# Part one's mixers in one block: in-projection, HGRN, mLSTM, banded attention and out-projection of a two-part transformer kernel

## The chip, the cores and the metric

The kernel runs on one core of one Trainium2 chip. The metric is the time of one execution on the device in microseconds (us); every time below is from the profile, the timed runs or the trace of one profiled execution. Engines: PE is TensorE, DVE is VectorE, ACT is ScalarE, POOL is GpSimd, SP issues the DMAs.

## The reference, cut to what matters

Two models follow one another on x (512 tokens, width 1024, fp32), each with two layers. Only part one's mixers are touched:

```python
for l in range(2):                       # first_block
    y = rms_norm(x) @ w_in[l] + b_in[l]  # 1024 -> 2824 columns
    # mq mk mv mo: 4 heads of 64; mi mf: 4 each; hq hf hi hg: 4 heads of 64
    # sq: 8 heads of 64, sk sv: 2 heads of 64
    qk    = silu(causal_conv4(mq|mk))
    m_out = head_norm(mlstm(qk, mv, mi, mf)) * sigmoid(mo)
    h_out = head_norm(hgrn2(silu(hq), hf, hi)) * silu(hg)     # decays exp(G_l - G_s), per feature
    s_out = banded_attention(rope(norm(sq)), rope(norm(sk)), sv, window 128, sinks)
    x = x + concat(m_out, h_out, s_out) @ w_out[l]
    x = x + square(relu(rms_norm(x) @ w_up[l])) @ w_down[l]   # 4096 wide
    x = x + gate(...)                                          # embedding gate
# second_block: two layers with three attentions and a gated MLP (5632 -> 2816)
```

## The kernel before, in words

**Products.** A weight matrix is cut into panels of at most 128 x 2048 fp32 (1 MB). SP loads a panel into one of `RAW` (3) buffers. ACT copies it rounded into one of three `high` buffers (`Panels.high`, L297), DVE puts the remainder into `low` (`Panels.low`, L309), and PE forms each product as three (high x high, high x low, low x high). `AHEAD` is 2: panel n+2 is split when work on panel n starts. `Panels.loads` lets the load of panel n wait until panel n-RAW has been split. A *feature group* is 24 matmuls of 128x512 (`project_feature`, L426), a *token group* 24 matmuls of 128x256 (`project_token`, L451). In part one's MLP the panels of `w_mod_2` are not split: DVE itself multiplies them (L1427, L1430), one beside each of the panels 1 to 6 of every eight.

**Part one's mixers** (`layer_one`, `mixers_one`, `project_heads`) are five stages, one block after the other. All engines meet between blocks.

1. In-projection: norm, then 12 panels in 9 feature and 28 token groups over six PSUM banks. Beside them DVE and ACT make the convolution and the gate sums.
2. mLSTM: 16 blocks (head, key tile). PE spreads the running maximum (L1041) and makes the scores (L1047), DVE adds the mask (L1097) and multiplies (L1106), ACT takes exp (L1069), PE sums over values (L1058). HGRN's gates are made beside them.
3. HGRN: two head pairs, ten levels each. Level lv cuts the tokens into blocks of 2B. `prepare` makes the spans of G against the middle of each block (L1151, then the sign L1153), ACT takes exp (L1223), `decay` multiplies all 512 queries and all 512 keys (L1164, L1165), PE makes 8 products (L1261), `keep` picks them under a mask (L1176). POOL rotates the window's queries and keys meanwhile. At a pair's end PE makes the results (L1237). Then queries and keys are turned (L555, L558).
4. Window attention: 32 units (head, query tile): scores (L467), maximum (L501), exp (L529), transposes (L478), copy (L538), result (L488), copy (L515).
5. Head scaling (L876, L882) and `project_heads`: transposes (L615), then 8 feature groups, each added to x (L886).

Part two's mixers (`layer_two`) are one block already: dense groups stand between the steps of attention pairs (`dense_at`), two heads of a pair use different rows of the array (L1821), and the dense groups use two banks.

Of the kernel before, what the change touches and what calls it, by code (L numbers as in the profile page):

```python
# [14 lines left out]
F32 = mybir.dt.float32  # L15
# [6 lines left out]
P = 128  # L22
# [7 lines left out]
RAW = 3  # L30
# [26 lines left out]
V_WIDTH = 64 + 6 * DC  # L57

R_BIAS, R_GM, R_GH, R_GQK, R_SINK = 0, 1792, 2048, 2304, 2944
# [19 lines left out]
def panels_one():  # L79


    k = lambda name, c0, n=PW: (name, 0, DC, [(c0, n, 0)], n)
    out = [k("w_in", 0), k("w_in", 256), ("w_in", 0, DC, [(C_GATES, MH, 0), (C_GATES + MH, MH, 32)], P)]
    out += [k("w_in", c) for c in (C_HQF, C_HQF + 256, C_MVO, C_MVO + 256, C_HIG, C_HIG + 256, C_SQ, C_SQ + 256, C_SKV)]
    out += [k("w_out", c) for c in range(0, D, PW)]
# [63 lines left out]
class AttentionSignals:  # L149
# [9 lines left out]


class TurnSignals:
    def __init__(self, s, name):
        self.t_ready = s(name)
        self.t_kept = s(name + "_kept")


class Unit:


    def __init__(self, q, k, cols, mask, scale, col, values, out, at=0, extra=None, sink=None):  # L170
        self.q, self.k, self.cols, self.mask, self.scale = q, k, cols, mask, scale
        self.col = col
        self.values, self.out = values, out
        self.at = at
        self.extra, self.sink = extra, sink
# [283 lines left out]
def attention_tensor(nc, pe, g, s, units):  # L459
    n = len(units)  # L460
    for i in range(n + 2):
        if i < n:
            u = units[i]
            if i >= 2:
                pe.wait_ge(s.max_ready, i - 1)
            b = g.bank[i % 2][:, 0:u.cols]
            ins = nc.tensor.matmul(b, u.q, u.k, start=True, stop=u.extra is None)  # L467
            if u.extra is not None:
                ins = nc.tensor.matmul(b, u.extra[0], u.extra[1], start=False, stop=True)
            ins.then_inc(s.scores_ready, 1)  # L470
        if 1 <= i <= n:
            j = i - 1
            u = units[j]
            pe.wait_ge(s.probs_ready, j + 1)
            if j >= 2:
                pe.wait_ge(s.turned_kept, j - 1)
            for m in range(u.cols // P):
                ins = nc.tensor.transpose(g.bank[2 + j % 2][:, m * P:(m + 1) * P], g.probs[:, j % 3, m * P:(m + 1) * P], g.ident)  # L478
            ins.then_inc(s.turned_ready, 1)
        if i >= 2:  # L480
            j = i - 2
            u = units[j]
            pe.wait_ge(s.turned_kept, j + 1)
            if j >= 2:
                pe.wait_ge(s.out_kept, j - 1)
            nb = u.cols // P
            for m in range(nb):
                ins = nc.tensor.matmul(g.bank[4 + j % 2][:, 0:2 * HD], g.turned[:, j % 2, m * P:(m + 1) * P], u.values[m],  # L488
                                       start=m == 0, stop=m == nb - 1)
            ins.then_inc(s.out_ready, 1)  # L490


def attention_vector(nc, dve, g, s, units):
    n = len(units)
    for i in range(n + 2):
        if i < n:
            u = units[i]
            dve.wait_ge(s.scores_ready, i + 1)
            if i >= 3:
                dve.wait_ge(s.probs_ready, i - 2)  # L500
            nc.vector.tensor_tensor_reduce(out=g.masked[:, i % 3, 0:u.cols], in0=g.bank[i % 2][:, 0:u.cols], in1=u.mask,  # L501
                                           scale=1.0, scalar=NEG, op0=ALU.add, op1=ALU.max,
                                           accum_out=g.rowmax[:, u.col:u.col + 1]).then_inc(s.max_ready, 1)
            dve.wait_ge(s.max_ready, i + 1)
            if u.sink is None:
                nc.vector.tensor_scalar(g.negmax[:, u.col:u.col + 1], g.rowmax[:, u.col:u.col + 1], -u.scale, None,
                                        ALU.mult).then_inc(s.neg_ready, 1)
            else:
                nc.vector.tensor_scalar(g.negmax[:, u.col:u.col + 1], g.rowmax[:, u.col:u.col + 1], u.sink, -u.scale,
                                        ALU.max, ALU.mult).then_inc(s.neg_ready, 1)  # L510
        if i >= 2:
            j = i - 2
            dve.wait_ge(s.out_ready, j + 1)
            at = units[j].at
            nc.vector.tensor_copy(units[j].out, g.bank[4 + j % 2][:, at:at + HD]).then_inc(s.out_kept, 1)  # L515


def attention_scalar(nc, act, g, s, units, beside=None):

    n = len(units)  # L520
    for i in range(n + 1):
        if i < n:
            u = units[i]
            if beside is not None:
                beside(i)
            act.wait_ge(s.neg_ready, i + 1)
            if i >= 3:
                act.wait_ge(s.turned_ready, i - 2)
            nc.scalar.activation(g.probs[:, i % 3, 0:u.cols], g.masked[:, i % 3, 0:u.cols], ACT.Exp,  # L529
                                 bias=g.negmax[:, u.col:u.col + 1], scale=u.scale,  # L530
                                 accum_out=g.rowsum[:, u.col:u.col + 1]).then_inc(s.probs_ready, 1)
        if i >= 1:
            j = i - 1
            act.wait_ge(s.turned_ready, j + 1)
            if j >= 2:
                act.wait_ge(s.out_ready, j - 1)
            c = units[j].cols
            nc.scalar.activation(g.turned[:, j % 2, 0:c], g.bank[2 + j % 2][:, 0:c], ACT.Copy).then_inc(s.turned_kept, 1)  # L538


def attention_buffers(nc, ctx, g, part):
    g.masked = ctx.enter_context(nc.sbuf_tensor(part + "_masked", [P, 3, S], F32))
    g.probs = ctx.enter_context(nc.sbuf_tensor(part + "_probs", [P, 3, S], F32))
    g.turned = ctx.enter_context(nc.sbuf_tensor(part + "_turned", [P, 2, S], F32))


def turn_tensor(nc, pe, g, s, blocks):

    for i, srcs in enumerate(blocks):
        if i >= BANKS:  # L550
            pe.wait_ge(s.t_kept, i - BANKS + 1)
        for m, src in enumerate(srcs):
            to = g.bank[1 + i % BANKS][:, m * P:(m + 1) * P]
            if src.shape[1] == P:
                ins = nc.tensor.transpose(to, src, g.ident)  # L555
            else:
                for r in range(0, P, HD):
                    ins = nc.tensor.matmul(to[r:r + HD, :], src, g.ident, start=True, stop=True)  # L558
        ins.then_inc(s.t_ready, 1)


def turn_scalar(nc, act, g, s, outs):
    for i, out in enumerate(outs):
        act.wait_ge(s.t_ready, i + 1)
        nc.scalar.activation(out, g.bank[1 + i % BANKS][:, :], ACT.Copy).then_inc(s.t_kept, 1)

def project_heads(nc, g, part, s, pan, l, columns, steps, before_scalar, before_vector, update):  # L570


    first = pan.first["w_out"]
    grp = Groups(["turn"] * DC + ["x"] * DC, {"turn": s("mix_low"), "x": s("x_updated")})
    full, high_ready = s("out_products"), s("mix_high")
    e = NormSignals(s, "mlp")
    with ExitStack() as ctx:
        mh = ctx.enter_context(nc.sbuf_tensor(part + "_mix_high", [P, DC, S], F32R))
        ml = ctx.enter_context(nc.sbuf_tensor(part + "_mix_low", [P, DC, S], F32R))
        with nc.Block() as block:  # L580
            @block.sync
            def _(sp):
                pan.loads(sp, l, first + AHEAD, first + 4 + AHEAD)

            @block.vector
            def _(dve):
                before_vector(dve)
                for c in range(DC):
                    dve.wait_ge(high_ready, c + 1)
                    nc.vector.tensor_tensor(ml[:, c, :], grp.bank(g, c)[:, :], mh[:, c, :].bitcast(F32), ALU.subtract).then_inc(s("mix_low"), 1)  # L590
                for c in range(DC):
                    if c % 2 == 0:
                        pan.low(dve, first + c // 2 + AHEAD)
# [1800 lines left out]
```

## Time and profile before

| | before |
|---|---|
| timed runs, us | 3276.65 median of 3 (3272.84 to 3308.1) |
| the profiled execution | 3276.12 us, its span 3274.3 us |
| PE / DVE / ACT / POOL busy | 3001.4 / 1696.6 / 1120.3 / 183.1 us |
| mean granted TensorE clock | 0.914 of full |

"Busy" is the time in which an instruction of that engine was under way; matmuls are pipelined and their ends are modelled, so a busy PE is not PE at its peak. The granted clock is the share of 2.4 GHz that the chip let TensorE have.

### The profile page before, as it was taken

Reading aid. Unit: us, or ns where it says so; the run is one execution under the profiler, and the core shown is the slowest. Engines: PE = TensorE matmul, PEld = TensorE weight load, DVE = VectorE, ACT = ScalarE, POOL = GpSimd, SP = SyncE. Lnnn points to the kernel's source line nnn. Section 1 sums busy time; section 2 is a strip of 40 time slices with the busy share of each in tenths; the row PEclk is TensorE's granted clock in tenths of the full one; section 3 lists DMA queues with packets and bytes.
Section 4 is the critical chain, followed back from the end, with each engine's and each line's share of the span. In section 5 each row is a group of like instructions: output and inputs, shape, how many; then the busy total and the mean of one; then the engine's idle time right before and its main releaser. Section 6 shows DMA issues by size and latency. Waiting matters only on the chain. (4 is left out here: it accounts for less than half of the span.)

```text
span 3274.3 us, 38168 instructions
## 1 busy us (share of the span) xinstructions
PE 3001.4 (92%) x14756; PEld 2451.6 (75%) x14756; DVE 1696.6 (52%) x2899; ACT 1120.3 (34%) x1851; POOL 183.1 (6%) x184
## 2 busy tenths in 40 slices
PE   5977899999889789999997899989999998999998
PEld 4956678888678576788886687778887787778886
DVE  3458555566553754655565553454342643454442
ACT  3252532223433424322234434433232434342231
POOL 0012000000200120000002000000000000000000
PEclk9955899999989556999998899999999999999999
DMA  4200034444142000344441310122321310122321
GB/s 167 94 13 1 14 116 155 154 155 167 33 143 78 1 1 14 123 161 160 160 155 34 127 64 28 39 79 77 115 80 51 136 51 28 52 78 79 108 87 61
DMA packets 42994, 281.39 MB, mean 86 GB/s; under 512 B 5944, under 2 KB 6200, under 8 KB 11704
## 3 DMA queue, kind: packets, MB, share of 16 engines
q1 hardware_dynamic: 42808, 278.86, 24.3%
q8 instruction: 122, 2.00, 0.2%
q14 instruction: 64, 0.52, 0.1%
HBM read 276.75 MB, written 2.10 MB: 85 GB/s over the span
## 5 line engine op out<-in xcount | busy, mean ns | idle before, releaser
L309 DVE TENSOR_TENSOR low_panels<-raw_panels,high_panels 128x2048 fp32r<-128x2048 f32 (+3 forms) x218 | 469.4, 2153 | 359.6 <-ACT high_panels L297 359.5
L297 ACT ACTIVATE high_panels<-raw_panels 128x2048 fp32r<-128x2048 f32 (+3 forms) x218 | 392.2, 1800 | 538.9 <-PE bank L1369 196.0
L426 PE MATMUL bank<-mlp_h_high,high_panels 128*128 128x512 f32 x1152 | 456.9, 397 | 0.0
L426 PE MATMUL bank<-mlp_h_low,high_panels 128*128 128x512 f32 x1152 | 454.9, 395 | 0.0
L426 PE MATMUL bank<-mlp_h_high,low_panels 128*128 128x512 f32 x1152 | 454.9, 395 | 0.0
L426 PEld LDWEIGHTS bank<-mlp_h_high,low_panels 128*128 128x128 f32 x1152 | 215.9, 187 | 52.8
L426 PEld LDWEIGHTS bank<-mlp_h_low,high_panels 128*128 128x128 f32 x1152 | 216.0, 188 | 51.8
L426 PEld LDWEIGHTS bank<-mlp_h_high,high_panels 128*128 128x128 f32 x1152 | 216.0, 188 | 51.7
L1369 PE MATMUL bank<-mlp_hid_high,high_panels 128*128 128x512 f32 x512 | 204.4, 399 | 0.0
L1369 PE MATMUL bank<-mlp_hid_low,high_panels 128*128 128x512 f32 x512 | 202.4, 395 | 0.0
L1369 PE MATMUL bank<-mlp_hid_high,low_panels 128*128 128x512 f32 x512 | 202.3, 395 | 0.0
L1430 DVE SCALAR_TENSOR_TENSOR mlp_mod_acc<-raw_panels,conditioning,mlp_mod_acc 128x256 f32<-128x256 f32 x336 | 165.1, 491 | 12.0
L1934 ACT ACTIVATE masked_scores<-masked_scores,stats 128x128 f32<-128x128 f32 (+3 forms) x160 | 81.3, 555 | 219.3 <-DVE stats L2038 219.3
L1261 PE MATMUL bank<-one_turned,one_probs 64*128 64x128 f32 (+1 forms) x512 | 99.9, 453 | 42.9 <-DVE one_probs L1165 42.9
L2161 PE MATMUL bank<-mlp_hid_high,low_panels 128*128 128x512 f32 x352 | 139.0, 395 | 0.0
L2161 PE MATMUL bank<-mlp_hid_high,high_panels 128*128 128x512 f32 x352 | 139.0, 395 | 0.0
L2161 PE MATMUL bank<-mlp_hid_low,high_panels 128*128 128x512 f32 x352 | 139.0, 395 | 0.0
L343 ACT ACTIVATE norm_buffers<-x 128x512 f32<-128x512 f32 x88 | 55.3, 630 | 242.4 <-DVE x L1451 66.4
L352 POOL TENSOR_TENSOR norm_buffers<-norm_buffers 128x512 f32<-128x512 f32 x11 | 16.3, 1480 | 2178.5 <-ACT norm_buffers L343 2178.5
L426 PE MATMUL bank<-h_high,high_panels 128*128 128x512 f32 x320 | 133.0, 416 | 0.2
L426 PE MATMUL bank<-h_low,high_panels 128*128 128x512 f32 x320 | 127.5, 398 | 0.0
L1261 PEld LDWEIGHTS bank<-one_turned,one_probs 64*128 64x128 f32 x512 | 86.9, 324 | 54.1 <-DVE one_probs L1165 53.4
(370 smaller groups left out, 5970.3 us busy)
## 6 DMA issues: line engine op xcount, KB each, us to landing
raw_panels<-in_w SPq DMA_DIRECT2D x238, 1024.0 KB, 4.9
raw_panels<-in_w SPq DMA_DIRECT2D x16, 384.0 KB, 3.2
raw_panels<-in_w SPq DMA_DIRECT2D x4, 960.0 KB, 4.7
raw_panels<-in_w SPq DMA_DIRECT2D x4, 768.0 KB, 4.2
row<-in_row SPq DMA_DIRECT2D x2, 1476.0 KB
x<-in_xT SPq DMA_DIRECT2D x1, 2048.0 KB, 7.5
raw_panels<-in_w SPq DMA_DIRECT2D x4, 512.0 KB, 7.7
mix<-in_rope SPq DMA_DIRECT2D x2, 1024.0 KB, 8.7
```

Of the source, the lines that this page charges most:

```text
L297: self.nc.scalar.activation(self.g.high[:, i % SPLIT, 0:raw.shape[1]], raw, ACT.Copy).then_inc(self.high_ready, 1)
L309: self.nc.vector.tensor_tensor(self.g.low[:, i % SPLIT, 0:w], raw, self.g.high[:, i % SPLIT, 0:w].bitcast(F32), ALU.subtract).then_inc(sel ...
L343: nc.scalar.activation(g.sq[:, c % 2, :], src, ACT.Square).then_inc(e.sq_ready, 1)
L352: nc.gpsimd.tensor_tensor(total, g.sq[:, 0, :], g.sq[:, 1, :], ALU.add).then_inc(e.sum_used, 2)
L426: ins = nc.tensor.matmul(bank[:, :], w[a][:, k, c0:c0 + P], rhs[b][:, k0 + k, :], start=first and k == 0 and j == 0, stop=last and k == kt ...
L1261: ins = nc.tensor.matmul(b[:, o:o + w], k[:, sx * P:(sx + 1) * P], q[:, t0 * P:t1 * P], start=True, stop=True)
L1369: ins = nc.tensor.matmul(b[:, :], w[a_][:, k, (m % 2) * P:(m % 2 + 1) * P], (uh, ul)[b_][:, k, :], start=k == 0 and j == 0, stop=k == DC - ...
L1430: ins = nc.vector.scalar_tensor_tensor(o, w[:, k, :], g.cond[:, k:k + 1], o, ALU.mult, ALU.add)
L1934: nc.scalar.activation(o, o, ACT.Exp, bias=g.negmax[:, 2 * i + m:2 * i + m + 1], scale=u.scale).then_inc(w.probs_ready, 1)
L2161: ins = nc.tensor.matmul(b[:, :], w[a_][:, k, (c % 2) * P:(c % 2 + 1) * P], (uh, ul)[b_][:, k0 + k, :], start=part == 0 and k == 0 and q = ...
```

## The change

Part one's mixers become one block per layer, written as part two's: each engine walks through one list of steps, and dense groups stand between them. `RAW` goes from 3 to 2 in the whole kernel. The dense groups use two banks (1 and 2): group i waits until group i-2 is evicted.

- **Order of the panels.** Forget, query, HGRN input, the two convolution panels, gates, mLSTM values, window keys and values, window queries (2), both gates of the outputs; then w_out as four panels of 4 row tiles x 512 columns.
- **Before the levels** (`n_before` = 8 groups): forget, query, HGRN input. ACT opens forget and query straight from PSUM (Abs, Sigmoid, Silu) and makes the logarithms; DVE scans.
- **Levels** (20 steps). The spans and the decay products are made for half of the tokens each: keys of the first half of a block, queries of the second, so that four operations of 256 elements take the place of four of 512. PE alternates between the two heads' rows. The two coarsest levels' copies go to ACT. Nine dense groups stand between the steps.
- **mLSTM** (16 steps): 20 token groups between them. The rotation moves from POOL to DVE, the squares of the heads stay on ACT.
- **Window attention in pairs** (16 pairs in 19 steps): DVE, ACT and PE as in part two, sinks and normalisation per pair. The eight mixed chunks are turned as they become ready, and 8 half groups of w_out ("first", 12 matmuls) stand between the steps; 8 more ("second") follow.
- Head gains are applied with the turned chunks, no longer by POOL.

The core of the diff (the order, and the loops of the three engines around the levels):

```diff
-RAW = 3
+RAW = 2
+        n_before = 8
+        dense_h = {1: [8], 3: [9], 5: [10], 7: [11], 9: [12], 11: [13], 13: [14], 15: [15], 17: [16]}
+        dense_m = {}
+        for i, j in enumerate(range(17, 37)):
+            dense_m.setdefault(2 * i // 3 if i < 12 else i - 4, []).append(j)
+        dense_w = {i: [first_groups[c]] for c, i in enumerate((7, 8, 9, 10, 12, 13, 16, 17))}
+        chunk_w = {2: [2], 3: [3], 5: [0], 6: [1], 7: [4], 11: [5], 15: [6], 18: [7]}
+        def dense_bank(i):
+            return bank[1 + i % 2]
...
+            @block.tensor            # products(k): waits d_decayed(k), and d_kept(k - 2)
+                for k in range(n_levels):
+                    products(k)
+                    if k == NL + 1:
+                        results(0)
+                    for i in dense_h.get(k, []):
+                        dense(i)
+                for j in range(n_blocks):
+                    if j == 2:
+                        results(1)
+                    if kt == 0:
+                        spread(hd)
+                    block_scores(j)
+                    if kt == 2 and hd >= 1:
+                        block_result(hd - 1)
+                    for i in dense_m.get(j, []):
+                        dense(i)
...
+                for p in range(n_pairs + 3):
+                    scores(p); result(p - 2); turn(p - 1)
+                    for c in chunk_w.get(p, []): turn_chunk(c)
+                    for i in dense_w.get(p, []): dense(i)
+                for i in second_groups: dense(i)
...
+            @block.scalar
+                for i in range(n_before):
+                    evict(i)
+                    if i == 1: forget_logs()      # Exp, Exp, Ln
+                    if i == 3: bound_logs()       # Abs, Abs, Exp, Ln
+                for k in range(n_levels):
+                    decay(k)                      # exp of the span of level k
+                    if k >= 1: keep_apart(k - 1)
+                    for i in dense_h.get(k, []): evict(i)   # waits for the group when ACT evicts it
+                    if k == 11: gate_logs()
+                    if k == 13: conv_open()
...
+            @block.vector
+                for i in range(n_before):
+                    evict(i)                      # at a panel's first group: pan.low(n + AHEAD)
+                    if i == 1: forget_sums(0)
+                    if i == 4: forget_sums(1)     # two scans, a memset
+                for k in range(n_levels):
+                    if k + 1 < n_levels: prepare(k + 1)
+                    decay(k)
+                    if k >= 1: keep(k - 1)
+                    if k == NL + 2: gather(0)
+                    for i in dense_h.get(k, []): evict(i)   # waits for the group when DVE evicts it
+                    if 9 <= k < 9 + CONV1: conv(k - 9)
+                    if k == 10: gates(0)
+                    if k == 14: gates(1)
...
+                def prepare(k):
+                    nc.vector.tensor_tensor(out[:, :, 0:B], ref, blk[:, :, 0:B], ALU.subtract)
+                    nc.vector.tensor_tensor(out[:, :, B:2 * B], blk[:, :, B:2 * B], ref, ALU.subtract).then_inc(s("d_span"), 1)
+                def decay(k):
+                    dve.wait_ge(s("d_decay"), j + 1)
+                    nc.vector.tensor_tensor(out[:, :, 0:B], out[:, :, 0:B], kv[:, :, 0:B], ALU.mult)
+                    nc.vector.tensor_tensor(out[:, :, B:2 * B], out[:, :, B:2 * B], qv[:, :, B:2 * B], ALU.mult).then_inc(s("d_decayed"), 1)
```

Groups 8 to 12 (convolution and gates, k = 1 to 9) are feature groups that ACT evicts; groups 13 to 16 (k = 11 to 17) are token groups that DVE evicts. The loops above are shortened; conditions on the first and last steps are left out.

## Rows read from the trace of the kernel before

**Rows 1.** The page: busy tenths of PE and granted clock in 40 slices.

```profile
PE   5977899999889789999997899989999998999998
PEclk9955899999989556999998899999999999999999
```

**Rows 2.** Stages of layer 0, layer 1's mixers, its window stage (start:end length, busy, PEclk).

```profile
36.00:176.60 140.60, 134.81 (x904) 124.60 (x904) 67.69 (x83) 45.48 (x44) 0.00 (x0) 1.00 0.36 126
176.60:233.00 56.40, 43.61 (x121) 27.26 (x121) 31.66 (x78) 27.39 (x45) 2.39 (x5) 0.52 0.00 1
233.00:339.00 106.00, 79.32 (x416) 71.39 (x416) 76.31 (x119) 33.05 (x112) 30.39 (x40) 0.51 0.00 1
339.00:388.50 49.50, 46.17 (x232) 30.61 (x232) 26.75 (x129) 35.40 (x163) 4.95 (x4) 0.97 0.00 1
388.50:444.10 55.60, 49.57 (x232) 42.01 (x232) 25.56 (x32) 17.44 (x21) 7.75 (x6) 0.94 0.22 76
908.00:1337.70 429.70, 375.96 (x1904) 312.14 (x1904) 228.06 (x440) 159.37 (x383) 45.47 (x55) 0.73 0.14 49
1211.90:1281.40 69.50, 66.94 (x232) 44.84 (x232) 26.73 (x129) 35.47 (x163) 4.95 (x4) 0.61 0.00 1
```

**Rows 3.** Timeline of one HGRN level (start, length in us).

```profile
265.50 3.09 PE L1261 MATMUL bank<-one_turned,one_probs 64*128 64x128 f32 x16 [0.65 <-DVE one_probs L1165]
266.57 0.68 DVE L1151 TENSOR_TENSOR norm_buffers<-proj 128x512 f32<-128x512 f32 x1
268.01 0.63 ACT L1223 ACTIVATE one_masked<-norm_buffers 128x512 f32<-128x512 f32 x1 [3.11 <-DVE norm_buffers L1153]
268.50 0.68 DVE L1165 TENSOR_TENSOR one_probs<-proj,one_masked 128x512 f32<-128x512 f32 x1
269.10 1.32 DVE L1176 COPY_PREDICATED proj<-k,bank 128x512 f32<-128x512 int32 x2
```

**Rows 4.** Timeline of DVE: evictions of two token groups, then two feature groups.

```profile
161.52 0.42 DVE L833 TENSOR_TENSOR proj<-bank,row 128x256 f32<-128x256 f32 x1 [2.46 <-PE bank L451]
164.40 0.42 DVE L833 TENSOR_TENSOR proj<-bank,row 128x256 f32<-128x256 f32 x1 [2.46 <-PE bank L451]
405.33 0.69 DVE L886 TENSOR_TENSOR x<-x,bank 128x512 f32<-128x512 f32 x1 [0.56 <-PE bank L426]
410.77 0.69 DVE L886 TENSOR_TENSOR x<-x,bank 128x512 f32<-128x512 f32 x1 [4.75 <-PE bank L426]
```

**Rows 5.** Timeline of part two: scores of one pair, 4 matmuls of 256 columns.

```profile
1936.74 0.92 PE L1821 MATMUL bank<-q_and_k 32*128 32x256 f32 x8
```

**Rows 6.** Timeline of ACT: a table load between Exp and Ln.

```profile
109.85 0.63 ACT L757 ACTIVATE neg_max<-neg_max 4x512 f32<-4x512 f32 x1
110.50 1.28 ACT L758 ACT_TABLE_LOAD   x1
111.79 0.63 ACT L758 ACTIVATE neg_max<-neg_max 4x512 f32<-4x512 f32 x1
```

**Rows 7.** Stretches of part two's mixers and of layer 1's first matmuls, with clock.

```profile
1900.00:1994.00 94.00, 92.83 (x685) 81.19 (x683) 43.25 (x140) 36.60 (x76) 0.00 (x0) 1.00 0.16 51
1994.00:1998.60 4.60, 2.48 (x23) 2.08 (x22) 3.79 (x9) 2.09 (x4) 0.00 (x0) 1.00 0.02 4
1998.60:2002.00 3.40, 3.40 (x13) 2.91 (x12) 0.83 (x5) 2.36 (x5) 0.00 (x0) 0.50 0.00 0
914.40:920.00 5.60, 5.53 (x13) 4.40 (x14) 5.05 (x6) 2.95 (x3) 0.00 (x0) 0.50 0.58 217
```

**Rows 8.** Timeline of PE in mLSTM and HGRN results, at the low clock.

```profile
202.36 4.61 PE L1047 MATMUL bank<-norm_buffers 64*128 64x512 f32 x6
222.60 4.53 PE L1058 MATMUL bank<-scratch,proj 128*128 128x65 f32 x20
329.93 1.49 PE L1237 MATMUL bank<-proj,scratch 128*128 128x64 f32 x6
```

**Rows 9.** Timeline of part one's MLP, and the landing time of its panel loads.

```profile
570.70 1.91 ACT L297 ACTIVATE high_panels<-raw_panels 128x2048 fp32r<-128x2048 f32 x1
571.91 3.61 DVE L1430 SCALAR_TENSOR_TENSOR mlp_mod_acc<-raw_panels,conditioning,mlp_mod_acc 128x256 f32<-128x256 f32 x7
575.43 2.28 DVE L309 TENSOR_TENSOR low_panels<-raw_panels,high_panels 128x2048 fp32r<-128x2048 f32 x1
DMA to landing us min/median/max: 4.7/5.2/5.9
```

More of the change, by code:

```diff
@@ L453, in project_token @@
     return ins
[L459 to L490, printed above, removed]
@@ L493, in attention_vector @@
[L493 to L515, printed above, removed]
@@ L518, in attention_scalar @@
[L518 to L538, printed above, removed]
@@ L541, in attention_buffers @@
[L541 to L559, printed above, removed]
@@ new lines, in layer_one @@
+        groups += [(12 + c // 4, "first", c) for c in range(DC)] + [(14 + c // 4, "second", c) for c in range(DC)]
+        panel_done = [sum(n <= p for n, _, _ in groups) for p in range(16)]
+        by_act = [sum(gr[1] in ("query", "conv", "gates") for gr in groups[:i]) for i in range(len(groups) + 1)]
+        by_dve = [sum(gr[1] in ("forget", "token") for gr in groups[:i]) for i in range(len(groups) + 1)]
+        by_sum = [sum(gr[1] in ("first", "second") for gr in groups[:i]) for i in range(len(groups) + 1)]
@@ new lines, in released, with level_bank, level_kept @@
+        def released(eng, i):
+            if i < 0:
+                return
+            if groups[i][1] in ("query", "conv", "gates"):
+                eng.wait_ge(kept_a, by_act[i + 1])
+            elif groups[i][1] in ("forget", "token"):
+                eng.wait_ge(kept_v, by_dve[i + 1])
+            else:
+                eng.wait_ge(x_updated, by_sum[i + 1])
+        def level_bank(k, hh_):
+            return bank[3 + (2 * k + hh_) % 4]
+        def level_kept(eng, k):
+            within = levels[k][1] <= TILE_LEVELS
+            n = 2 * sum((lv <= TILE_LEVELS) == within for _, lv in levels[:k + 1])
+            eng.wait_ge(d_kept if within else ao_kept, n)
@@ new lines, in _ @@
+                dve.wait_ge(s("in_gains"), 16)
+                norm_vector(nc, dve, g, e, x, vec[:, V_GIN:V_GIN + DC], hh, hl,
+                            before={1: lambda: pan.low(dve, 0), 4: lambda: pan.low(dve, 1)})
+                dve.wait_ge(s("in_vectors"), 48)
+                bounds(0)
+                st(nc.vector.memset(qk_raw[:, :, 0:3], 0.0))
+                bounds(1)
+                for i in range(n_before):
+                    evict(i)
+                    if i == 1:
+                        forget_sums(0)
+                    if i == 4:
+                        forget_sums(1)
@@ new lines, in _ @@
+                keep(n_levels - 1)
+                gates(2)
+                for j in range(n_blocks + 1):
+                    if j < n_blocks:
+                        block_weights(j)
+                    if j >= 1:
+                        block_probs(j - 1)
+                    if j == 3:
+                        gather(1)
+                    if j in (7, 11, 15):
+                        finish((j - 7) // 4)
+                    for i in dense_m.get(j, []):
+                        evict(i)
+                    if j == 8:
+                        head_squares(hi_out, 0, region(3592, 1024))
+                    if 11 <= j < 15:
+                        rotate(j - 11)
```

1315 lines of the change are left out of this document (685 added, 630 removed).

## The prediction, as put on record before the result

> **What bounds the kernel now.** I read the page's slices first [rows 1]: PE is busy nearly everywhere, and the granted clock is at its full level (2.4 GHz) except in two dips, slices 3 to 5 and 14 to 16, which are the mixers of part one's two layers. The table of stages [rows 2] then says what each stage is worth. The reader is to see three things there. The in-projection (140.6 us) is PE at full clock with idle DVE and ACT. mLSTM and HGRN (56.4 + 106.0 us) have the clock at half and PE waiting: this is where overlap could pay. The window stage costs 49.5 us in layer 0, where the clock stayed up, and 69.5 us in layer 1, where it did not. From the norm's first work to the last sum into x the mixers take 408.1 us in layer 0 (36.0 to 444.1) and 429.7 us in layer 1, together 837.8 us. Nothing outside these stretches is edited, apart from RAW. I price four new phases per layer by the program order of the diff, at full clock first, then with the clock.
>
> **Prices.** One HGRN level is 3.7 us of DVE (0.7 + 0.6 + 0.6 + 0.6 + 1.2) while PE needs 3.1 us at the low clock and ACT 0.63 [rows 3]. An operation of 512 elements takes 0.68 and the next starts 0.60 after it [rows 3]; one of 256 elements takes 0.42 [rows 4], 0.34 by the same overlap. So the halved level costs DVE 4 x 0.34 + 1.2 = 2.6 us. A token group is 2.88 us and a feature group 5.44 us [rows 4]. Level products: two heads on different rows overlap in part two, 4 matmuls of 256 columns in 0.92 us [rows 5], where one after another they would take 1.5 (the 3.1 us of a level's 8 x 128 columns at the low clock, halved); so 0.9 us a level at full clock, 1.8 at the low one. A table load is 1.28 us [rows 6].
>
> **Phase A, up to the first decayed level.** The first two groups end 20.0 us after the start, as now. Then two banks replace six, and group 2 waits for ACT and DVE: bounds with two table loads (3.0), the high copy (1.9), Abs 0.6, a load 1.3, Sigmoid 0.6, DVE 0.6, which is 6.7 us of idle PE. Two query groups 10.9, two token groups 5.8. Group 6 needs group 4 evicted, and before that DVE takes a `low` whose `high` stands on ACT behind the bound logarithms (Silu 0.6, two Abs 1.1, Exp and Ln of 1024 with two loads 4.7, the copy 1.9), then 2.3 + 0.4: some 5.5 us more of idle PE. Two token groups 5.8 and the chain evict, prepare, exp, decay 2.4. Sum 57 at full clock; the two gaps bring the low clock, which costs 3 to 7 more. I take 61, bounds 57 and 64. Here the Trainium skill would say more: ScalarE: Activation LUTs, "What ACT_TABLE_LOAD costs", puts a switch at 2.66 us, a load of 1.28 and a drain of 1.38. The trace disagrees with the second half: Exp ends at 110.48, the load starts at 110.50 and Ln at 111.79 [rows 6], and six loads by the page would make phase A 8 us longer.
>
> **Phase B, the levels.** What matters is who waits for a dense group. At k = 1, 3, 5, 7, 9 ACT evicts it, and the exp of level k+1 stands behind that on ACT. So from decay(k): products 0.9, dense 5.5, PE's tail 0.2, evict 0.6, exp 0.6, decay 0.7, and then the even level's DVE work keep, prepare, decay 2.6: 11.1 us per two levels, 56 for five. At k = 11 to 17 DVE evicts, and prepare and decay of k+1 stand behind: 0.9 + 2.9 + 0.2 + 0.4 + 1.3 + 2.6 = 8.3 us per two levels, 33 for four. On top, not covered by anything: three of four convolution steps 3 x 2.6, the second gate step 4.6 (two scans), results(0) 40 records of 0.21 us at the low clock [rows 8], 4.3 at full, the gather 0.6, the last level's products 0.9. Sum 107. DVE alone would need 20 x 2.6 + 10 + 5 + evictions and lows of about 13 = 80, PE 39 + 18 + 4: neither bounds it, the round trip does. **The clock.** Per two levels PE idles 2.2 us, works 0.9, idles 1.7. In part two a stretch of 4.6 us with 2.1 us idle was followed by a stretch at half clock [rows 7], and layer 1's first full-row matmuls ran 5.6 us at half clock before it rose [rows 7]. So I let each dense group start low: 1.9 to 2.9 us for the group and 0.5 for products, 3.3 x 9 = 30. B is 137; bounds 107 and, low all the way, 158 (5 x 6.3 + 4 x 3.8 + 4.3 more).
>
> **Phase C, mLSTM.** PE: 20 x 2.88 = 57.6; scores 9 (5.4 - 0.6 for a head at the low clock, halved, x 4) and spreads 4; results of three heads 3 x 2.2 and results(1) 4.2 [rows 8]. Sum 81. DVE has 16 x 1.0 + 8 + five lows 11.5 + four rotations of 3 + squares and ends 7 = 55 of these, but crowded in steps 8 to 15, and two banks give little slack: 5 more, 86. PE is over 90% busy, so the clock should hold. The rotation that POOL did beside DVE costs 12 us of DVE here, under cover of token groups; without that cover it would be 12. Bounds 81 to 92.
>
> **Phase D, window and out-projection.** Turning queries and keys 7 (6.7 us with the last results now, between rows 2's HGRN stage and its end). A unit of the window stage takes 1.44 us on average (49.5 us less its ends, 32 units), limited by its chain of engines; a pair needs the same chain once with two heads: 2.9 us, over 18 steps 52. A "first" group is 2.7 us of PE, of which some 0.8 hides in each step: 8 x 1.9 = 15. Steps 1 and 3 carry DVE's head norms (7.5) behind Sigmoid, Silu and Sqrt with four table loads: 12. Chunks 5. Eight "second" groups 22. Sum 113, bounds 105 (chain shorter, as twice 1.33) and 133 (+20, what the low clock does to the stage in layer 1 [rows 2]).
>
> **RAW.** With two raw buffers the load of a split panel starts when the `low` of the panel before it in that buffer ends. In the MLP's crowded periods of 11.65 us that is 6.2 us after the first modulation product, it lands 4.7 to 5.9 later [rows 9], at 10.9 to 12.1; `high` is wanted at 10.8 and ends by 14.0, and the `low` is due only at 15.5, behind the next 3.9 us of modulation. So the slack is 1.5 us and the price zero. In part two the period is 10.9 us with one panel and the slack is larger.
>
> **Sum.** 61 + 137 + 86 + 113 = 397 a layer, 794 for both against 837.8: 43.8 us less. The profiled execution took 3276.1 us (its span 3274.3), within 0.6 us of the median 3276.65, so 3276.1 - 43.8 = 3232.
>
> **Rivals.** (1) *The clock holds at full*, as it does in nearly all of part two's mixers, which have the same form (1.00 over 94 us [rows 7]). Then A is 57, B 107, C 81, D 105: 350 a layer, 3138 us. For it: bursts of 6.4 us, longer than the waits. TensorE: Matmul & The Clock Gate, section "HAM oscillation", has the oscillation arise where bursts are shorter than the waits between them; by that the clock would hold here, and the result would be this rival's. Against it: 2.1 us of idle time in 4.6 sufficed [rows 7]; B has 3.9 in 4.8. (2) *Slower: the clock stays at half through the levels and the pairs*, as it did for the whole of layer 1's window stage although PE counted as busy for 66.94 of 69.50 us [rows 2]. B 158, D 133, A 64, C 88: 443 a layer, 3324 us. It decides against the change from 22 us a layer above my sum, that is when half of what lies between my B and D and these ends is lost. Against it: in layer 1's start dense work brought the clock up after 5.6 us [rows 7], and the dense groups are such work. (3) *Panels become late.* If with two raw buffers a load landed later than 7.4 us after its start, each us over is paid in 48 periods; 8.5 us would give 3232 + 53 = 3285. Two loads already share the queue now and land within 5.9. (4) *The phases overlap as planned but ACT's or DVE's fixed order costs more than my chains*, some 20 us a layer: 3272.
>
> **How the numbers follow.** My forecast 3232 (reach 3190 to 3275) 0.50; rival 1 (3110 to 3190) 0.22; rival 2 0.14; rival 3 0.04; rival 4 0.10. Two in ten may be left out: the range is 3135 to 3310. A measurement of this kernel tells about 1% from no change. Faster by over 1% (below 3244): 0.22 + 0.38 = 0.60; within 1%: 0.12 + 0.10 + 0.02 = 0.24; slower: 0.16.
>
> **What would show it.** After, two levels with a feature group between them are 11 to 15 us apart and PE's idle time there goes to the decayed products of DVE, whose own wait goes to ACT's exp; the clock in the levels is 0.6 to 0.8 on average; the third group of each layer starts some 6 us after the second ends; C has PE busy over 90% at full clock; panel loads land as before and MLP periods stay at 11.65 us. I am wrong if the exp of level k+1 is found ahead of the dense group, if the clock holds, if ACT's table loads in the window steps make a pair longer than 3 us, or if MLP periods grow.

## The result and the profile after

The changed kernel takes 3254.47 us (median of 20 runs, one of which, at 9696 us, stands apart), the kernel before 3282.97 (20 runs, taken beside them); the ratio is 0.9931, 95% interval 0.9906 to 0.9957. That is a gain of 0.7%, which I would have called no change, where I forecast 1.4%. The time lies inside my range. The profiled execution took 3257.54 us (span 3255.7), 18.6 less than that of before.

The page of the changed kernel, busy tenths of PE and granted clock in 40 slices:

```profile
PE   4779889999967788999997998999998998999998
PEclk9769789999988888999998999999999999999999
```

Against [rows 1] the two deep dips are gone. In their place stand longer, shallower ones: 0.6 to 0.9 in slices 2 to 6, 0.8 in 12 to 16. The stages, start:end length, busy time of each engine, and PEclk after the five engines; layer 0, then layer 1, each cut at the first work after the norm, the first level's products, the first spread of mLSTM, the turning of the window's queries, the first "second" group, and the last sum into x:

```profile
35.70:95.80 60.10, 43.71 (x200) 37.17 (x200) 32.25 (x43) 34.56 (x37) 0.00 (x0) 0.86 0.32 115
95.80:229.40 133.60, 95.12 (x554) 79.94 (x553) 70.09 (x138) 32.59 (x45) 0.00 (x0) 0.72 0.09 32
229.40:335.70 106.30, 98.79 (x623) 84.38 (x621) 48.28 (x107) 31.69 (x108) 0.00 (x0) 0.87 0.15 50
335.70:429.40 93.70, 76.79 (x428) 60.01 (x429) 51.90 (x198) 43.03 (x104) 0.00 (x0) 0.80 0.07 23
429.40:454.00 24.60, 23.98 (x107) 18.76 (x105) 11.06 (x12) 8.82 (x11) 7.75 (x6) 1.00 0.25 85
915.60:973.80 58.20, 40.93 (x200) 34.51 (x200) 32.24 (x43) 34.97 (x37) 0.00 (x0) 0.83 0.33 112
973.80:1099.00 125.20, 86.01 (x553) 71.51 (x552) 69.95 (x138) 32.60 (x45) 0.00 (x0) 0.78 0.10 34
1099.00:1200.10 101.10, 93.62 (x622) 80.76 (x621) 48.21 (x107) 31.67 (x108) 0.00 (x0) 0.92 0.15 53
1200.10:1292.30 92.20, 73.31 (x428) 56.69 (x429) 51.86 (x198) 43.06 (x104) 0.00 (x0) 0.85 0.07 24
1292.30:1316.60 24.30, 23.67 (x105) 18.46 (x104) 11.01 (x12) 8.60 (x10) 7.75 (x6) 1.00 0.25 86
```

| us | predicted | layer 0 | layer 1 |
|---|---|---|---|
| A, up to the first level | 61 | 60.1 | 58.2 |
| B, levels | 137 | 133.6 | 125.2 |
| C, mLSTM | 86 | 106.3 | 101.1 |
| D, window and out-projection | 113 | 118.3 | 116.5 |
| sum | 397 | 418.3 | 401.0 |
| before [rows 2] | | 408.1 | 429.7 |

819.3 us against 837.8: 18.5 us less, all of the 18.6 of the whole execution. So on balance nothing moved outside the mixers, and the question is what stands in them: B waits as foreseen, C is 15 to 20 us too long.

One period of two levels in B, layer 1 of the changed kernel, timelines of PE, DVE and ACT (L695 products, L1147 and L1148 decayed products, L1162 keep, L1136 and L1137 prepare, L925 exp):

```profile
1013.54 1.65 PE L695 MATMUL bank<-arena 64*128 64x128 f32 x16 [2.09 <-DVE arena L1148]
1016.09 2.08 PE L695 MATMUL bank<-arena 64*128 64x128 f32 x16 [0.91 <-DVE arena L1148]
```
```profile
1012.72 0.42 DVE L1147 TENSOR_TENSOR arena<-arena 128x256 f32<-128x256 f32 x1 [6.46 <-ACT arena L925]
1013.06 0.42 DVE L1148 TENSOR_TENSOR arena<-arena 128x256 f32<-128x256 f32 x1
1013.40 1.33 DVE L1162 COPY_PREDICATED arena<-k,bank 128x512 f32<-128x512 int32 x2
1014.62 0.41 DVE L1136 TENSOR_TENSOR arena<-arena 128x256 f32<-128x256 f32 x1
```
```profile
1012.07 1.14 ACT L925 ACTIVATE arena<-arena 128x512 f32<-128x512 f32 x2
```

PE ends its feature group at 1011.4 and waits 2.09 us, the tail, ACT's eviction, the exp and the decayed product, one behind the other, exactly the 0.2 + 0.6 + 0.6 + 0.7 of the prediction. DVE, which had been idle for 6.46 us beside the dense group, could have made that product long before: its input waited on ACT behind the eviction. The next such pair begins 13.8 us later.

### The profile page after: what moved, and what is told of

Read it like the earlier page. It is cut to its first block and busy times, and to the rows that moved or that the text cites. A ratio compares the mean times of both kernels' runs of the same rounds, so it can differ in the third digit from the quotient of the medians.

```text
span 3255.7 us, 37966 instructions
## 1 busy us (share of the span) xinstructions
PE 2933.1 (90%) x14756; PEld 2392.4 (73%) x14756; DVE 1667.8 (51%) x3011; ACT 1107.3 (34%) x1691; POOL 107.9 (3%) x88
## 5 line engine op out<-in xcount | busy, mean ns | idle before, releaser
L445 PE MATMUL bank<-high_panels,h_high 128*128 128x256 f32 x704 | 215.5, 306 | 12.0 <-DVE arena L1100 11.4
L445 PE MATMUL bank<-low_panels,h_high 128*128 128x256 f32 x704 | 205.7, 292 | 0.0
L445 PE MATMUL bank<-high_panels,h_low 128*128 128x256 f32 x704 | 204.8, 291 | 0.0
L1419 PE MATMUL bank<-mlp_hid_high,high_panels 128*128 128x512 f32 x512 | 204.5, 399 | 0.0
L420 PE MATMUL bank<-h_high,low_panels 128*128 128x512 f32 x496 | 203.3, 410 | 0.0
L1419 PE MATMUL bank<-mlp_hid_low,high_panels 128*128 128x512 f32 x512 | 202.4, 395 | 0.0
L1419 PE MATMUL bank<-mlp_hid_high,low_panels 128*128 128x512 f32 x512 | 202.3, 395 | 0.0
L445 PEld LDWEIGHTS bank<-high_panels,h_high 128*128 128x128 f32 x704 | 142.3, 202 | 28.4 <-issue 15.6
L445 PEld LDWEIGHTS bank<-low_panels,h_high 128*128 128x128 f32 x704 | 142.3, 202 | 1.5 <-issue 1.4
L445 PEld LDWEIGHTS bank<-high_panels,h_low 128*128 128x128 f32 x704 | 141.5, 201 | 0.0
```

The lines of the kernel that those rows point to most:

```text
L420: ins = nc.tensor.matmul(bank[:, :], w[a][:, k, c0:c0 + P], rhs[b][:, k0 + k, :], start=first and k == 0 and j == 0, stop=last and k == kt ...
L445: ins = nc.tensor.matmul(bank[:, 0:n], rhs[b][:, k, t * P:(t + 1) * P], w[a][:, k, :], start=k == 0 and j == 0, stop=k == DC - 1 and j == 2)
L1419: ins = nc.tensor.matmul(b[:, :], w[a_][:, k, (m % 2) * P:(m % 2 + 1) * P], (uh, ul)[b_][:, k, :], start=k == 0 and j == 0, stop=k == DC - ...
```

## The experiments

Each was run beside the kernel before; ratios are to it. The diffs are shortened; `...` stands for lines left out. "B", "C" and "D" are the stages of the table, D without the "second" groups from here on (93.7 and 92.2 us in the changed kernel).

**Two raw buffers alone, in the kernel before.**

```diff
-RAW = 3
+RAW = 2
```

> The kernel before with two raw buffers instead of three, nothing else. Prediction's step (slack 1.5 us in each MLP period, price zero): within 5 us of the kernel before, MLP periods 11.65 us as before, landing median of the 1 MB panels near 5. Rival 3 (panels become late): each us past the slack is paid in 48 periods, so 30 to 60 us slower. A third possibility is the old in-projection, where panels follow one another every 11 us with two to split: some us a layer lost there and nothing in the MLP.

Measured: 3277.16 us, ratio 1.0007 (0.9971 to 1.0043). A timeline of ACT in its first MLP shows that the price is paid in slack only:

```profile
594.12 1.91 ACT L297 ACTIVATE high_panels<-raw_panels 128x2048 fp32r<-128x2048 f32 x1 [0.98 <-DMA raw_panels<-in_w]
606.46 1.92 ACT L297 ACTIVATE high_panels<-raw_panels 128x2048 fp32r<-128x2048 f32 x1 [1.67 <-DMA raw_panels<-in_w]
```

ACT now waits up to 1.67 us for the load, and the `low` behind it still starts every 11.64 us (597.78, then 609.42), the old period. Rival 3 is out, and the old in-projection of layer 0 takes 140.9 us, from the norm's spread to mLSTM's first one, where it took 140.6.

**The levels one further ahead.** No exp and no decayed product stands behind a dense group any more.

```diff
 scalar
-                for k in range(n_levels):
-                    decay(k)
+                decay(1)
+                for k in range(n_levels):
+                    if k + 2 < n_levels:
+                        decay(k + 2)
 vector
-                prepare(0)
+                prepare(1)
                 for k in range(n_levels):
-                    if k + 1 < n_levels:
-                        prepare(k + 1)
-                    decay(k)
+                    if k + 2 < n_levels:
+                        prepare(k + 2)
+                    if k + 1 < n_levels:
+                        decay(k + 1)
...
-                    for i in dense_h.get(k, []):
+                    for i in dense_h.get(k - 1, []):
                         evict(i)
```

> The changed kernel, with the level work one level further ahead: DVE prepares level k+2 and multiplies level k+1 in step k, ACT takes the exp of level k+2 in step k, and DVE adds the rows of a token group one step later, so no exp or decayed product stands behind a dense group. If the round trip (dense group, ACT's eviction, exp, decay) sets phase B, as the prediction has it, the 2.09 us that PE waits after each feature group goes to under 0.3, a pair of levels takes 7.5 to 9 us at full clock where it took 13.9, and phase B falls from 133.6 and 125.2 us to 90 to 105: the kernel takes 3185 to 3215 us. If the clock alone sets it (half speed in the dense groups whatever PE waits for), the waits go but a pair stays over 12 us: 3235 to 3250. If DVE's total work sets it, the waits move to the products: 3240 to 3255.

Measured: 3172.43 us, ratio 0.9699 (0.9651 to 0.9748), 13 us below the least that I expected. The timeline of PE and the stage of B in either layer:

```profile
932.13 2.06 PE L695 MATMUL bank<-arena 64*128 64x128 f32 x32
939.91 2.06 PE L695 MATMUL bank<-arena 64*128 64x128 f32 x32
```
```profile
95.98:185.68 89.70, 77.07 (x553) 66.50 (x553) 69.69 (x138) 32.54 (x45) 0.00 (x0) 0.87 0.14 48
922.52:1011.18 88.66, 76.67 (x553) 66.20 (x552) 69.57 (x138) 32.53 (x45) 0.00 (x0) 0.87 0.14 48
```

Two levels' products now follow each other without a wait, and a period is 7.78 us at full clock: PE's own 5.8 + 2.0. The work is the same (DVE 69.7 us busy against 70.0), so B's 44 and 37 us were order, not work, and in them is what the low clock behind each wait had cost. The round trip set phase B. C is left as it was in kind, 99.6 and 102.9 us.

**ACT's part of it alone.** In step k ACT takes the exp of level k+1 ahead of the eviction; DVE as changed.

```diff
-                    decay(k)
+                    if k + 1 < n_levels:
+                        decay(k + 1)
```

> The changed kernel with ACT's part alone of the run-ahead: in step k ACT takes the exp of level k+1 before it evicts the dense group of step k; DVE's order is as changed. If ACT's eviction before the exp is what holds the feature pairs, their wait of 2.09 us goes; the exp of level k+2 still stands behind the eviction, so a pair keeps some 1.2 us of wait and takes 8.5 to 10 us where it took 13.9, while the token pairs, held by DVE's own order, stay: 20 to 27 us a layer, 3200 to 3215 us. If DVE's order is the limit, under 8 us a layer: over 3235.

Measured: 3229.45 us, ratio 0.9850 (0.9788 to 0.9911), between the two expectations. The timeline of PE shows the pair as expected, with one wait of 1.00 us left and the next pair's start 9.05 us after this one's:

```profile
981.37 1.16 PE L695 MATMUL bank<-arena 64*128 64x128 f32 x16
983.53 1.16 PE L695 MATMUL bank<-arena 64*128 64x128 f32 x16 [1.00 <-DVE arena L1149]
990.42 0.72 PE L695 MATMUL bank<-arena 64*128 64x128 f32 x8
```

What I missed lies behind it. In layer 1 the part of B up to results(0) fell from 69.7 to 50.7 us, while the rest rose from 55.5 to 62.3, since the 40 result matmuls now met the half clock (8.4 us in place of 4.7), and C rose from 101.1 to 106.4. In layer 0 of the changed kernel these stretches already took that long (62.3 and 106.3 us, the result matmuls 8.8). A gain in one stretch moved the clock's steps in the next.

**More DVE work in each level**, as full-size spans and products would bring it.

```diff
                 def prepare(k):
+                    nc.vector.tensor_tensor(region(14368 + 448 * (j % 2), 448), G[:, c, 0:448], G[:, c, 0:448], ALU.subtract)
                 def decay(k):
+                    nc.vector.tensor_tensor(region(12304 + 448 * (j % 2), 448), G[:, c, 0:448], G[:, c, 0:448], ALU.subtract)
```

> The changed kernel, with two more DVE operations of 448 elements in each of the 18 decayed levels (one when level k+1 is prepared, one in decay(k)), 1.1 us a level, about what four operations of 512 elements cost above four of 256 (4 x 0.26). Their results are used nowhere. If the round trip sets phase B, the part of a level's DVE work that lies between ACT's exp and the next products is paid: 0.54 after each dense group and 1.1 in the other level, some 1.6 us for each of nine pairs, 14 us a layer, more at the low clock: 3280 to 3295 us. If DVE's work were covered by the dense groups, under 5 us a layer: below 3265.

Measured: 3294.37 us, ratio 1.0049 (1.0014 to 1.0083), 40 us above the changed kernel. The timeline of PE: the two waits of a pair are 2.62 and 1.98 where they were 2.09 and 0.91, that is 0.53 and 1.07 more, the amount of DVE work put between the exp and the products.

```profile
1018.79 1.65 PE L695 MATMUL bank<-arena 64*128 64x128 f32 x16 [2.62 <-DVE arena L1150]
1022.42 1.87 PE L695 MATMUL bank<-arena 64*128 64x128 f32 x14 [1.98 <-DVE arena L1150]
```

B grew by 14.2 us in layer 0 and 24.2 in layer 1 (147.8 and 149.4), where I expected 14 a layer. Some 8 us of the 24.2 are probably the clock's: in this run both layers look like the long pattern described further down (C is 105.4 and 105.5 us), which in the changed kernel only layer 0 had. So in this order the half-size products are worth 30 to 40 us. By this stand-in the change without them would have ended 0.5% above the kernel before; the full-size products themselves were not run.

**Filled waits in the levels.** Nine matmuls whose results are used nowhere, before the products of each of levels 2 to 17.

```diff
                 for k in range(n_levels):
+                    if 2 <= k < 18:
+                        for _ in range(9):
+                            nc.tensor.matmul(bank[0][:, 0:256], hh[:, 0, 0:P], hh[:, 0, 0:256], start=True, stop=True)
                     products(k)
```

> The changed kernel, with nine more matmuls of 128 x 256 columns into an unused bank before the products of each of the levels 2 to 17 (1.0 us at full clock, 2.0 at half; their result is used nowhere). If the low clock costs phase B some 25 us a layer, as the prediction has it, and PE's waits bring it, the clock stays up, and B takes 105 to 115 us in place of 125 to 134 although PE has 16 us more work: 3215 to 3235. If the waits are what costs and the clock little, B grows by up to what does not fit in them: 3250 to 3275.

Measured: 3225.86 us, ratio 0.9862 (0.9813 to 0.9910); windows of B, both layers:

```profile
96.49:212.01 115.52, 94.21 (x698) 81.51 (x697) 69.90 (x138) 32.60 (x45) 0.00 (x0) 0.90 0.11 37
956.96:1072.27 115.31, 94.11 (x698) 81.42 (x697) 69.90 (x138) 32.60 (x45) 0.00 (x0) 0.90 0.11 37
```

With 144 matmuls more in each layer, B is 18 and 10 us shorter, and the clock 0.90 where it was 0.72 and 0.78. The waits' second price, the low clock behind them, is real. Both layers now show the same B. C is 104.6 and 104.5 us, in layer 1 3.4 more than in the changed kernel.

**The rotation of mLSTM, two tiles on POOL.** DVE rotates tiles 0 and 1 in steps 11 and 14, POOL the others; the squares of the HGRN heads move to step 3.

```diff
-                    if j == 8:
+                    if j == 3:
                         head_squares(hi_out, 0, region(3592, 1024))
-                    if 11 <= j < 15:
-                        rotate(j - 11)
+                    if j in (11, 14):
+                        rotate({11: 0, 14: 1}[j])
...
+            # POOL, once the roots are inverted: the same operations for t in (2, 3)
```

> The changed kernel, with two of the four token tiles' rotations on POOL and two on DVE in steps 11 and 14, and the squares of the HGRN heads in step 3 in place of step 8. If DVE's crowding in steps 8 to 15 of mLSTM makes PE wait (2.5 + 4.7 us in layer 1) and the waits bring the low clock (some 7 us more on results and token groups), phase C falls from 106 and 101 us to 88 to 94: 3225 to 3240 us. If the size of C comes from PE's own work, C stays over 97: 3248 to 3258. If POOL slows DVE or ends after step 15, the turning of the window's queries begins later: 3255 to 3270.

Measured: 3230.57 us, ratio 0.9878 (0.9830 to 0.9926). The time came out as expected, C did not: 99.3 and 96.6 us, with two waits of 2.4 us left. C gave 7.0 and 4.5 us, half of the 24 between the medians; the rest may be the patterns described further down, since the unedited changed kernel itself reached 3239.22 in a later series, and the two intervals overlap. So this run shows the waits' cause only in part, and the next one settles it. What the rotation did in the changed kernel, timelines of DVE and PE in layer 1 (L1238 to L1248 is one rotation, L1208 and L1214 are the mask and the products that PE needs):

```profile
1180.03 2.29 DVE L303 TENSOR_TENSOR low_panels<-raw_panels,high_panels 128x2048 fp32r<-128x2048 f32 x1 [2.40 <-ACT high_panels L291]
1182.24 0.42 DVE L1100 TENSOR_TENSOR arena<-bank,row 128x256 f32<-128x256 f32 x1
1182.57 0.81 DVE L1238 TENSOR_TENSOR arena<-arena,small 128x640 f32<-128x640 f32 x1
...
1185.44 0.56 DVE L1208 TENSOR_TENSOR arena<-bank,k 128x384 f32<-128x384 f32 x1
1185.91 0.68 DVE L1214 SCALAR_TENSOR_TENSOR arena<-bank,arena 128x512 f32<-128x512 f32 x1
```
```profile
1186.65 1.22 PE L741 MATMUL bank<-norm_buffers 64*128 64x256 f32 x2 [4.72 <-DVE arena L1214]
1187.80 4.53 PE L754 MATMUL bank<-arena 128*128 128x65 f32 x20
```

DVE first waits 2.40 us for ACT's `high`, then makes `low` (2.3), an eviction and a rotation (2.9), and only then the product that PE has been waiting for. PE's next 20 value matmuls run at half clock: 4.53 us, where the first head's 20, behind no wait, took 2.45.

**Both, with all four tiles on POOL** from step 10 on: the levels one further ahead, and the rotation as below, shown against the run with two tiles on POOL.

```diff
-                    if j in (11, 14):
-                        rotate({11: 0, 14: 1}[j])
+                    if j == 10:
+                        rotate()               # inverts the roots only
...
-                        pe.wait_ge(s("w_rotated"), NT)
+                        pe.wait_ge(s("w_rotated_pool"), NT)
```

> The changed kernel with the level work one level further ahead, as in the run before, the squares of the HGRN heads in step 3 of mLSTM, and all four rotations on POOL from step 10 on (6.2 us a tile there, 25 us, where C has 45 us left). If what is left of phase C above PE's own 87 us (from the run with two tiles on POOL: 96.6 us less 4.8 of waits and 4.9 of low clock behind them) is DVE's crowding, C falls to 87 to 90 us in both layers, from 99.6 and 103.0, and the kernel takes 3142 to 3155 us. If POOL's tiles end late or slow DVE, the turning waits: C over 93 us, 3160 to 3175.

Measured: 3144.37 us, ratio 0.9594 (0.9535 to 0.9653). Windows of C, in the run with the levels ahead alone, then in this one:

```profile
185.68:285.26 99.58, 92.07 (x622) 79.46 (x621) 48.29 (x107) 31.69 (x108) 0.00 (x0) 0.93 0.16 54
1011.18:1114.13 102.95, 95.42 (x623) 82.50 (x621) 48.29 (x107) 31.69 (x108) 0.00 (x0) 0.90 0.15 52
182.92:271.31 88.39, 86.57 (x623) 74.24 (x621) 42.22 (x83) 31.99 (x108) 21.04 (x32) 1.00 0.18 60
998.39:1086.78 88.39, 86.56 (x622) 74.24 (x621) 42.21 (x83) 32.00 (x108) 21.03 (x32) 1.00 0.18 60
```

C is 88.4 us in both layers at a clock of 1.00: 25.8 of the 28.1 us between the two runs are there. PE's own work is nearly all of it: 20 token groups of 2.92 (58.4), scores of 2.94 for each of four heads (11.8), four spreads (4.2), results(1) 4.5, three value results of 2.26 (6.8), together 85.7; then 1.3 us of waiting for POOL's last tile at the end, and 1.4 of smaller waits and of the last level's products.

**Filled waits elsewhere, on top of it.** 36 matmuls before the third group of A, 9 before levels 11, 12, 14 and 16, 4 to 16 small ones in the window steps without dense work.

```diff
                 for i in range(n_before):
+                    if i == 2:
+                        fill(36, bank[0])
                     dense(i)
                 for k in range(n_levels):
+                    if k in (11, 12, 14, 16):
+                        fill(9, bank[0])
...
+                    if 2 <= p < 7:
+                        fill_f32(16 if p == 2 else 4, bank[1])
...
```

> The kernel of the run beside it (levels ahead, rotation on POOL), with matmuls whose results are used nowhere put into PE's waits: 36 of 256 columns before the third group of phase A (in a wait of 6.4 us), 9 before the products of levels 11, 12, 14 and 16, and 4 to 16 of 128 x 128 in the window steps without dense work. If the low clock behind each wait still costs what it does in these stretches (2 us in A, 8 in B, 4 to 8 in D), 20 to 30 us less than the run beside it; if the filling is longer than the waits or the clock falls anyway, 0 to 15 us more.

Measured: 3129.63 us, ratio 0.9547 (0.9489 to 0.9606): 14.7 us less than the run beside it, where I expected 20 to 30. B took 4.8 and 2.7 us less, D 2.1 and 3.4, A 1.3 and 0.7. D's clock rose to 0.96, where it had been 0.78 and 0.80, for some 3 us: the pairs are a chain of ACT and DVE, and PE's speed weighs little there.

**Once more, for the intervals.**

> The changed kernel once more, without an edit, as the measure for the versions beside it: 3250 to 3258 us.

> The version with levels ahead, rotation on POOL and filled waits once more, for its interval: 3126 to 3133 us.

Measured: the changed kernel 3239.22 us, ratio 0.9887 (0.9839 to 0.9935), outside what I expected; the version with everything 3130.14, ratio 0.9550 (0.9504 to 0.9596). Windows of the changed kernel's layer 0 this time:

```profile
93.96:219.08 125.12, 85.96 (x553) 71.54 (x552) 69.95 (x138) 32.58 (x45) 0.00 (x0) 0.78 0.10 34
219.08:320.20 101.12, 93.65 (x623) 80.83 (x621) 48.25 (x107) 31.70 (x108) 0.00 (x0) 0.92 0.16 53
```

Its layer 0 now looks like layer 1 did: 125.1 and 101.1 us, 400.0 in all down to the end of the second groups, where that took 417.3. A layer comes in two patterns of the same code, 17 us apart, by where the clock's steps fall, and the runs of the first series fall into three groups, 4 at 3235 to 3238, 9 at 3251 to 3258 and 6 at 3267 to 3281. The profiles show what the first two are: at 3237.84 no layer has the long pattern, at 3257.54 one has it. That the third is both layers is likely by its distance, but no profile shows it. The kernel before has two patterns as well, window stages of 49.5 and 69.5 us [rows 2]. In the versions without waits for DVE in C both layers take 88.4 or 88.5 us there; their B and D still differ by up to 2 us between layers and runs.

**The mLSTM gate's Sigmoid earlier**, from window step 0 to step 13 of mLSTM, in the version with everything.

```diff
+                    if j == 13:
+                        act.wait_ge(kept_v, by_dve[at_panel[11]])
+                        nc.scalar.activation(mo, mo, ACT.Sigmoid).then_inc(s("gates_open"), 1)
...
                     if p == 0:
                         act.wait_ge(kept_v, by_dve[at_panel[12]])
-                        nc.scalar.activation(mo, mo, ACT.Sigmoid).then_inc(s("gates_open"), 1)
```

> The same version with the Sigmoid of the mLSTM gate taken from window step 0 to step 13 of mLSTM, where ACT is idle most of a step. If ACT's table loads and gates in window steps 0 to 2 hold the first pairs (PE waited 4.5 us for a copy of ACT there), phase D falls by 1.5 to 2.5 us a layer: 3125 us. If the exp of mLSTM's step 14 then comes late, behind two table loads and 1.1 us of Sigmoid, C grows by 1 to 2 us a layer and the time stays or rises to 3133.

Measured: 3128.79 us, ratio 0.9540 (0.9494 to 0.9586), no difference from the run beside it. D is 89.3 and 90.4 us, where the run beside it has 90.1 in both layers and the same version in the series before had 91.9 and 90.1; C stayed at 88.4. Neither of the two expectations shows. The version beats both kernels of this case by 4.6% and 3.4% (3128.79 against 3275.88 and 3239.22), no more than the version without it.

## Why the prediction was off

**What failed is the size of phase C.** The step reads "PE is over 90% busy, so the clock should hold", with 81 us of PE and 5 of crowding. PE was busy for 93% of C, and the clock fell all the same, in layer 1 behind each of two waits for DVE. The 101.1 us there are 85.7 of PE's own work (I had 81: a head's scores take 2.94 us at full clock and not 2.25, which is most of it), 7.5 of waits (2.5, 4.7 and 0.3), and some 8 of low clock behind them: two value results of 4.3 us for 2.3, two token groups of 3.9 and 4.3 for 2.9, and smaller ones. Layer 0 has the same waits (2.5, 4.7 and 0.3) and 5 us more of low clock, 3 of them at the start: up to the second block's scores it takes 10.9 us, in layer 1 8.0. I named the crowd in steps 8 to 15 and priced it by DVE's average load of 55 us in 86, where the order inside a step decides: `low` and a rotation ahead of the product that PE waits for. Over both layers C is 35 us above the prediction, more than the whole miss of 25: A and B came in 4 and 15 below, D 9 above, so that part of the miss was cancelled by luck. That C's waits come from DVE's work is shown by the run with all four tiles on POOL, where they go with it and C falls to 88.4.

**What held.** A: 60.1 and 58.2 for 61, with the wait before the third group at 6.4 us for 6.7. B: 133.6 and 125.2 for 137, by parts 71.3 and 69.7 up to results(0), where my chains with the low clock make 73, and 62.3 and 55.5 behind it for 64. One price in it was off without effect: the products of a level take 1.16 us at full clock and 2.08 at the low one, not 0.9 and 1.8, and the wait behind them was shorter by as much. B's mechanism, the round trip through ACT's eviction, is shown by the run without it (89 us) and by the run that lengthens it (0.53 and 1.07 us more of waits for 0.54 and 1.08 of work). That the clock adds to it is shown by the filled waits. D: 118.3 and 116.5 for 113, inside its bounds. The lower of these, 105, does not follow from its own figures: 18 steps of twice 1.33 are 48 us where I had 52, which gives 109. RAW at nothing: 1.0007.

**The rivals.** Rival 1, the clock at full, did not come: B had 0.72 and 0.78. I had weighed the rule of the Trainium skill, TensorE: Matmul & The Clock Gate, section "HAM oscillation", which has the oscillation arise where bursts are shorter than the waits between them. In this trace the bursts were the longer ones: waits of 2.09 and then 0.91 to 1.42 us stood beside dense groups of 5.8 us or more, and the clock fell in four of the five periods with a feature group. The same page's section "A second HAM failure mode: psum-queue depth-cycling" tells of a kernel in which frequent short idle times between groups of matmuls made the clock go up and down, and the trace agrees with that one. Rival 2, half clock throughout, did not come either. Rival 3 is excluded. Rival 4, "some 20 us a layer" lost to the fixed order of ACT and DVE, is the nearest: the miss is 12.6 us a layer, and C is its place.

**The comparison itself** was worth as much as the miss. My sum set 397 us a layer against 408.1 and 429.7, one short and one long pattern of the kernel before. The changed kernel's layers are 401.0 and 418.3: like for like it gains 7 and 11 us, and with both layers short it takes 3236 to 3238. A median of a few runs says which patterns came, as much as what the code costs.

**Where the expected gain went.** The in-projection had run at full clock with PE busy for 134.8 of 140.6 us [rows 2]. Spread between chained steps, its groups ran at half speed for a part (7.2 us for a feature group in the period shown, 5.8 in the version with the levels ahead), and each of them held up the chain that it was to cover. The overlap paid once the chain stood ahead of the groups.

## What to carry to other kernels

When dense groups are put between the steps of a chain, look at what each engine's queue holds behind the group's eviction: the chain's next step must be issued ahead of it, or the group is added to the chain and not hidden by it. Here this order was worth 82 us and the merging itself 28, by the medians of the first series; with the later one's median of the changed kernel, 3239.22, they are 67 and 37. Price each step by the order inside it and not by the engine's mean load, and look for two patterns of the same code before comparing layers or medians.

## What the runs showed of the hardware

- A wait costs twice. In C of the changed kernel the 20 value matmuls behind a wait of 4.72 us took 4.53 us, behind none 2.45.
- Matmuls whose results are used nowhere pay in such waits: 144 of them in each layer made stage B 18 and 10 us shorter. The whole kernel was 28 us below the changed kernel's first median, and 13 below its later one.
- DVE and POOL slow each other at times. In the run with the rotation on POOL a `low` of DVE took 3.49 us, not 2.28, and beside it POOL's four small products 3.23, not 1.28 (timelines of POOL and of DVE, layer 0):

```profile
252.03 1.28 POOL L657 TENSOR_TENSOR arena<-arena,cos_sin 128x80 f32<-128x80 f32 x4
257.10 3.23 POOL L657 TENSOR_TENSOR arena<-arena,cos_sin 128x80 f32<-128x80 f32 x4
```
```profile
255.68 3.49 DVE L303 TENSOR_TENSOR low_panels<-raw_panels,high_panels 128x2048 fp32r<-128x2048 f32 x1 [2.40 <-ACT high_panels L291]
```

The Trainium skill, GPSIMD Engine Reference, section "Specifications", has the two engines share their ways into SBUF when DVE's instruction has two inputs there; that fits these rows: the `low` of DVE reads both its inputs from SBUF. The rows also show how: `low` began while POOL still had 1.3 us of its product of 128x640 (L651) to do, and took 1.2 us longer than alone. Then the first of POOL's four small products took 2.29 us, not 0.35, and ended 0.2 us after `low`. Two other `low` operations of this run, each beside 1.2 us of POOL's work elsewhere in the kernel, took 2.29 us, so not every overlap costs.
